# Second-row x turned by VectorE and exchanged through HBM at five stage boundaries, in place of TensorE transposes

## Chip, cores and metric

One core of one Trainium2 chip runs the whole program. The metric is device time in microseconds, the median of several runs. Before the change: 942.03 us, median of 3 runs (939.99 to 943.75).

## The reference

A two-layer decoder trunk on x of 256 rows by 1024 columns, all in float32. Each layer does

```
h = h + 0.5 * swiglu(rms_norm(h, g1), w_gate, w_up, w_down)     # FFN, inner width 2816
h = h + mixer(rms_norm(h, g2))
h = h + 0.5 * swiglu(rms_norm(h, g3), w_gate, w_up, w_down)
```

The mixer of layer 0 is causal differential attention (w_qkv 1024 x 3072, w_o 1024 x 1024). Between the layers one shared K/V is made from rms_norm(h, kv_norm). The mixer of layer 1 is sliding-window attention with sinks (w_q, w_o 1024 x 1024) that reads it. A last rms_norm gives the output.

## The kernel before

The 256 rows are two blocks of 128: pos 0, the first rows, and pos 1, the second rows. Four FFNs, the QKV projection, two attentions, the shared K/V and the w_q and w_o projections run one after the other. Weights come in 157 units of 128 x 2048 elements (1 MB); four are held in SBUF (UNITS_HELD). To get float32 accuracy each operand is split in a high part (float32r) and a low part: ScalarE copies raw into w_hi (L1192), VectorE subtracts to get w_lo (L1536), and TensorE sums three products, hi*hi, hi*lo and lo*hi. One pass over one unit for one block of rows in `columns_pass` (L427) is 12 matmuls of 128x128 by 512 columns. The order of all work is written out by hand for each engine, and each engine runs strictly in that order; semaphores join them. SyncE issues all loads from one queue: the load of unit u waits until VectorE has split unit u-4.

TensorE contracts over partitions, so x must be turned: xT_hi and xT_lo hold the 1024 columns on partitions, 8 tiles by 256 rows. At the end of a stage, VectorE adds the block's result to x (`residual`, L1567) and multiplies by the norm's gain (`gained`, L1557, writes xn and raises s_xn). TensorE transposes xn in eight 128x128 pieces into two PSUM banks (`x_transposes`, L482), ScalarE copies the banks to xT_hi (`x_hi`, L1217), and VectorE writes xT_lo (`x_lo`, L1542). The factor 1/rms comes in later, with the silu, the bias or the copy of the projection.

At each boundary u0 is the first weight unit of the next stage. TensorE first runs the first rows over u0 to u0+3, four passes, and then the second rows over the same units. The second rows' result of the old stage is done only when the new stage begins, so their residual, gain, transposes and parts are made while TensorE runs the first rows' four passes. The transposes stand behind the third of these passes, and `x_ready` before the first pass of the second rows. VectorE's order there is residual(1), split u0+2, split u0+3, gained(1) (`boundary`, `next_phase`).

Before the third FFN (U_FFN1_1) two normalisations of the same x are turned, one for the shared K/V (kept in the hT buffers) and one for the FFN. `kv_pass` (L599) makes K and V with 24 matmuls of 256 columns for each block.

The FFN's inner activations h are turned in another way already. VectorE transposes h in 32x32 blocks (`h_turned`, L1599, STREAM_TRANSPOSE of 128x512 into the silu buffer), SyncE writes 256 KB to a buffer in HBM (`h_out`, L878), waits for its landing, and reads it back with four transfers of 64 KB into xn, one for each group of 32 partitions (`h_in`, L886). ScalarE then copies to hT_hi (L1238) and VectorE makes hT_lo (L1607). The loads of later units stand between these transfers in SyncE's order.

Of the kernel before, what the change touches and what calls it, by code (L numbers as in the profile page):

```python
# [30 lines left out]
F32 = mybir.dt.float32  # L31
# [7 lines left out]
P = 128  # L39
# [87 lines left out]
def trunk(nc, a, out):  # L127
    with ExitStack() as ctx:
# [3 lines left out]
        def sem(name):  # L132
            return ctx.enter_context(nc.semaphore(name))
# [77 lines left out]
        landed = [xn[:, pos, 0:BANK] for pos in range(NPOS)]  # L211

# [42 lines left out]
        s_hT_lo = [sem(f"s_hT_lo{i}") for i in range(NPOS)]  # L255
        s_hipart = sem("s_hipart")
# [132 lines left out]
        def _(pe):  # L389
# [401 lines left out]
            for part in range(3):  # L791
                u0 = U_QKV + 4 * part
                for pos in range(NPOS):
                    for i in range(4):
                        if part == 0 and pos == 0 and i == 3:
                            x_transposes("ln_mix_0", 1)
                        if part == 0 and pos == 1 and i == 0:
                            x_ready("ln_mix_0", 1)
# [39 lines left out]
            for pos in range(NPOS):  # L838
                for i in range(4):
# [4 lines left out]
                    if pos == 0 and i == 3:  # L844
                        x_transposes("ln_mix_1", 1)
                    if pos == 1 and i == 0:
                        x_ready("ln_mix_1", 1)
# [18 lines left out]
        def _(sp):  # L866
# [21 lines left out]
            def ffn(f, u0, w_gate, w_up, w_down, l, *vectors):  # L888
# [18 lines left out]
                for k in range(2 if f == 0 else 0, 8):  # L907
                    unit(u0 + k, k % 2, CH * (k // 2))

# [49 lines left out]
            def columns(u0, n_chunks, w):  # L959

                view = w.rearrange("(k p) n -> p k n", p=P)
                for c in range(n_chunks):
                    for half in range(2):
                        u = u0 + 2 * c + half
                        dst = raw[:, slot(u), :].rearrange("p (k n) -> p k n", k=4)
                        load(u, [(dst[:, 2 * i:2 * i + 2, :],
                                  view[:, 4 * half + 2 * i:4 * half + 2 * i + 2, BANK * c:BANK * (c + 1)])
                                 for i in range(2)])

# [21 lines left out]
            ffn(0, U_FFN1_0, a["ffn1_w_gate"], a["ffn1_w_up"], a["ffn1_w_down"], 0, "ln_mix_0", "ln_ffn2_0", "kv_norm")  # L991
            columns(U_QKV, 6, a["a_w_qkv"][0])
            rows(U_WO_A, 4, a["a_w_o"][0])
            vector("ln_ffn1_1")
            ffn(1, U_FFN2_0, a["ffn2_w_gate"], a["ffn2_w_up"], a["ffn2_w_down"], 0, "ln_mix_1")
# [3 lines left out]
            ffn(2, U_FFN1_1, a["ffn1_w_gate"], a["ffn1_w_up"], a["ffn1_w_down"], 1, "b_b_q", "b_b_o")  # L999
            columns(U_WQ, 2, a["b_w_q"][0])  # L1000
            rows(U_WO_B, 4, a["b_w_o"][0])
            vector("ln_ffn2_1")
            ffn(3, U_FFN2_1, a["ffn2_w_gate"], a["ffn2_w_up"], a["ffn2_w_down"], 1, "final_norm")
# [174 lines left out]
        def _(act):  # L1178
# [43 lines left out]

            def ffn(f, u0, name, aside=None):
# [21 lines left out]
                def turn_of(g, turn=None):  # L1245
                    if g == 0:
                        if name == "ln_ffn1_1":
                            x_hi("kv_norm", 1)
                        x_hi(name, 1)
                    silu_gate(0, 1, g, turn)  # L1250
                    split(u0 + 4 * g + 4, turn)
# [144 lines left out]
            x_hi("ln_mix_0", 1)  # L1396
            projection(0, 0, 1, q_a[:, 0, BANK:D])
            split(U_QKV + 4)
# [85 lines left out]
            x_hi("ln_mix_1", 1)  # L1484
            transposed(qT[:, 0:4, own(0)], 4, ("qT_b", 0, 0))
            split(U_WO_B)
# [35 lines left out]
        def _(dve):  # L1522
# [35 lines left out]

            def residual(key, pos, scale, u_last):
# [11 lines left out]
            def boundary(key, u_last, u0, name, scale=0.5):  # L1571
# [14 lines left out]
            def ffn(f, u0, name):  # L1586
# [28 lines left out]
                def turn_of(g, turn=None):  # L1615
                    if g == 0:
                        if name == "ln_ffn1_1":
                            x_lo("kv_norm", 1)
                        x_lo(name, 1)
                    mul(0, 1)  # L1620
                    if g == 0 and name == "ln_ffn1_1":
# [130 lines left out]
            def next_phase(layer, u0, name):  # L1752
# [11 lines left out]
                residual(("wo", layer), 1, 1.0, u0 - 1)  # L1764
                split(u0 + 2)
                split(u0 + 3)
                gained(name, 1, ("wo", layer))
# [47 lines left out]
            x_lo("ln_mix_0", 1)  # L1815
# [83 lines left out]
            x_lo("ln_mix_1", 1)  # L1899
            queries(0, 1)  # L1900
            split(U_WO_B)
# [67 lines left out]
```

## Time and profile before

| | |
|---|---|
| median of 3 runs | 942.03 us (939.99 to 943.75) |
| the profiled execution | 941.22 us, its span 939.3 us |
| PE busy | 925.9 us, 99% |
| DVE, ACT, POOL busy | 556.7, 459.9, 87.0 us (59%, 49%, 9%) |
| PE L482, all transposes | 2.7% of the chain that ended last |
| DMA | 193.37 MB, 206 GB/s mean |
| mean granted TensorE clock | 0.997 |

PE is TensorE's matmuls, PEld its weight loads, DVE VectorE, ACT ScalarE, POOL GpSimd, and SPq SyncE's queue of DMA issues. A timeline row has the start in us, the duration, the engine, the line of the kernel, the operation, output and input, and in brackets the idle time before it with what ended it. A matmul row shows 0.39 us although the next one starts 0.227 us later: matmuls are pipelined, so starts are to be compared, not durations.

### The profile page before, as it was taken

The page shows a single profiled execution, that of the slowest core. Times are in us where ns is not written, and L with a number is a line of the kernel's source. Part 1 is how long each engine was busy: PE and PEld are TensorE (multiplying, and loading weights), DVE is VectorE, ACT ScalarE, POOL GpSimd, SP SyncE. Part 2 cuts the span into 40 slices and gives each one's busy share as a digit, 9 for nine tenths or more (in the row PEclk, how much of TensorE's full clock was granted, in tenths as well). Part 3 has the DMA queues.
Part 4 walks back from the last instruction along what each step waited for, and adds up shares of the span by engine and source line. Part 5 has one row for each costly group of instructions (what it writes and reads, how often), then busy time and mean ns, then how long its engine had stood idle before and what let it go on. Part 6 is the DMA issues. An engine that isn't in the chain of part 4 may idle for free.

```text
span 939.3 us, 11549 instructions
## 1 busy us (share of the span) xinstructions
PE 925.9 (99%) x4338; PEld 759.6 (81%) x4338; DVE 556.7 (59%) x537; ACT 459.9 (49%) x581; POOL 87.0 (9%) x168
## 2 busy tenths in 40 slices
PE   8999999999999999999999999999999999999996
PEld 7878888888877888888888888888876788888885
DVE  5566663554587666664466666644568766666542
ACT  6354643455676544444343445443447654444431
POOL 1510000024311100000004000000031010000000
PEclk9999999999999999999999999999999999999998
DMA  9798884554532678885564788864641468888521
GB/s 313 190 311 264 293 280 177 179 179 179 202 106 76 191 246 251 251 280 197 188 207 146 227 247 254 306 208 180 217 163 51 129 191 251 248 242 290 201 77 45
DMA packets 149947, 193.37 MB, mean 206 GB/s; under 512 B 8712, under 2 KB 121376, under 8 KB 149904
## 3 DMA queue, kind: packets, MB, share of 16 engines
q1 hardware_dynamic: 149568, 192.45, 62.4%
q0 software_dynamic: 320, 0.34, 0.5%
q8 instruction: 28, 0.46, 0.2%
q14 instruction: 15, 0.12, 0.0%
q10 hardware_dynamic: 16, 0.00, 0.0%
HBM read 181.22 MB, written 11.53 MB: 205 GB/s over the span
## 4 chain that ended last, share of the span: by engine, by line
PE 90%; DMA 3%; ACT 3%; DVE 3%; SPq 1%; POOL 1%; issue 0%; POOLq 0%; DVEq 0%; ACTq 0%
PE bank L427 54%; PE bank L464 20%; PE bank L468 10%; PE bank L482 3%; DMA h_bounce<-silu 2%; DMA raw<-in_ffn_w_up 1%; DVE w_lo L1536 1%; ACT w_hi L1192 1%; PE bank L622 1%; PE bank L599 1%; PE bank L675 1%; ACT silu L1330 0%; ACT h L1330 0%; PE bank L653 0%; ACT w_hi L1344 0%; SPq L886 0%
## 5 line engine op out<-in xcount | busy, mean ns | idle before, releaser
L1536 DVE TENSOR_TENSOR w_lo<-raw,w_hi 128x2048 fp32r<-128x2048 f32 x154 | 351.8, 2293 | 191.2 <-ACT w_hi L1192 191.1
L1192 ACT ACTIVATE w_hi<-raw 128x2048 fp32r<-128x2048 f32 x154 | 295.3, 1919 | 178.4 <-PE bank L468 87.6
L427 PE MATMUL bank<-w_hi,xT_hi 128*128 128x512 f32 x832 | 326.1, 392 | 1.8 <-DVE w_lo L1536 0.8
L427 PE MATMUL bank<-w_hi,xT_lo 128*128 128x512 f32 x832 | 324.0, 389 | 0.0
L427 PE MATMUL bank<-w_lo,xT_hi 128*128 128x512 f32 x832 | 323.9, 389 | 0.0
L427 PEld LDWEIGHTS bank<-w_hi,xT_hi 128*128 128x128 f32 x832 | 156.2, 188 | 36.4 <-issue 2.2
L427 PEld LDWEIGHTS bank<-w_hi,xT_lo 128*128 128x128 f32 x832 | 156.2, 188 | 32.7
L427 PEld LDWEIGHTS bank<-w_lo,xT_hi 128*128 128x128 f32 x832 | 156.3, 188 | 31.6
L464 PE MATMUL bank<-w_hi,hT_hi 128*128 128x512 f32 x348 | 136.4, 392 | 0.0
L464 PE MATMUL bank<-w_lo,hT_hi 128*128 128x512 f32 x348 | 135.4, 389 | 0.0
L468 PE MATMUL bank<-w_hi,hT_lo 128*128 128x512 f32 x348 | 107.2, 389 | 0.0
L468 PEld LDWEIGHTS bank<-w_hi,hT_lo 128*128 128x128 f32 x348 | 65.3, 188 | 13.7
L1238 ACT ACTIVATE hT_hi<-xn 128x512 f32 (+1 forms) x40 | 25.0, 625 | 104.7 <-DMA xn<-h_bounce 104.7
L464 PEld LDWEIGHTS bank<-w_hi,hT_hi 128*128 128x128 f32 x348 | 65.3, 188 | 13.3
L464 PEld LDWEIGHTS bank<-w_lo,hT_hi 128*128 128x128 f32 x348 | 65.4, 188 | 13.2
L1591 DVE SCALAR_TENSOR_TENSOR h<-bank,rstd,silu 128x256 f32<-128x256 f32 x88 | 42.0, 479 | 43.5 <-ACT silu L1232 43.5
L1031 POOL TENSOR_SCALAR ms<-ss 128x1 f32<-128x1 f32 x13 | 5.6, 429 | 668.8 <-ACT junk L1210 668.7
L1232 ACT ACTIVATE silu<-bank,rstd 128x256 f32<-128x256 f32 x88 | 40.2, 460 | 49.1 <-PE bank L427 49.0
L1607 DVE TENSOR_TENSOR hT_lo<-xn,hT_hi 128x512 f32 (+1 forms) x40 | 27.6, 689 | 51.2 <-ACT hT_hi L1238 51.2
L1210 ACT ACTIVATE junk<-x 128x1024 bf16<-128x1024 f32 x13 | 13.7, 1050 | 44.1 <-DVE x L1567 44.0
L1567 DVE SCALAR_TENSOR_TENSOR x<-bank,x 128x512 f32<-128x512 f32 x22 | 14.2, 686 | 31.9 <-PE bank L468 31.9
L1599 DVE STREAM_TRANSPOSE silu<-h 128x512 f32<-128x512 f32 x40 | 28.4, 711 | 1.3
(157 smaller groups left out, 579.1 us busy)
## 6 DMA issues: line engine op xcount, KB each, us to landing
raw<-in_ffn_w_down SPq DMA_DIRECT2D x88, 512.0 KB, 5.1
raw<-in_ffn_w_gate SPq DMA_DIRECT2D x86, 512.0 KB, 4.6
raw<-in_ffn_w_up SPq DMA_DIRECT2D x86, 512.0 KB, 6.0
raw<-in_a_w_qkv SPq DMA_DIRECT2D x24, 512.0 KB, 4.7
h_bounce<-silu SPq DMA_DIRECT2D x40, 256.0 KB, 5.8
xn<-h_bounce SPq DMA_DIRECT2D x160, 64.0 KB, 3.3
raw<-in_a_w_o SPq DMA_DIRECT2D x8, 512.0 KB, 3.9
raw<-in_b_w_q SPq DMA_DIRECT2D x8, 512.0 KB, 5.3
```

What stands on the lines that cost most here:

```text
L427: mm = nc.tensor.matmul(bank[b][:, :], xs[:, kt, own(pos)], ws[:, slot(u), cols], start=(kt == 0 and i == 0), stop=(kt == KT - 1 and i == 2))
L464: nc.tensor.matmul(bank[acc(pos, j)][:, :], lhs_hi[:, kt, own(pos)], ws[:, slot(u), cols], start=(kt == 0 and i == 0), stop=False)
L468: mm = nc.tensor.matmul(bank[acc(pos, j)][:, :], lhs_lo[:, kt, own(pos)], w_hi[:, slot(u), cols], start=False, stop=(kt == n_kt - 1))
L482: mm = nc.tensor.transpose(bank[b][:, P * i:P * (i + 1)], src, ident[:, :])
L1192: nc.scalar.activation(w_parts(u)[0], raw[:, slot(u), :], ACT.Copy).then_inc(s_hi, 1)
L1232: nc.scalar.activation(silu_of(pos, j, g), bank[acc(pos, j)][:, 0:CH], ACT.Silu, scale=rstd[:, pos:pos + 1]).then_inc(s_silu, 1)
L1238: nc.scalar.activation(hT_hi[:, bass.ds((g + turn) * 4, 4), own(pos)].rearrange("p t (q s) -> p t q s", q=4), landed[pos].rearrange("p (q ...
L1536: nc.vector.tensor_tensor(lo, raw[:, slot(u), :], hi.bitcast(F32), ALU.subtract).then_inc(s_lo, 1)
L1567: nc.vector.scalar_tensor_tensor(out=x[:, pos, cols], in0=bank[acc(pos, j)][:, :], scalar=scale, in1=x[:, pos, cols], op0=ALU.mult, op1=AL ...
L1591: nc.vector.scalar_tensor_tensor(out=h[:, pos, CH * j:CH * (j + 1)], in0=bank[b][:, CH:2 * CH], scalar=rstd[:, pos:pos + 1], in1=silu_of(p ...
L1599: nc.vector.transpose(turned[pos].rearrange("p (q t s) -> p t q s", q=4, t=4), h[:, pos, :].rearrange("p (t q s) -> p t q s", t=4, q=4)).t ...
L1607: nc.vector.tensor_tensor(hT_lo[:, tile, own(pos)].rearrange("p t (q s) -> p t q s", q=4), landed[pos].rearrange("p (q t s) -> p t q s", q ...
```

## The change

At five boundaries (ln_mix_0, ln_ffn2_0, ln_ffn1_1, ln_mix_1, ln_ffn2_1) the second rows are turned the way h is. VectorE works on halves of 512 columns: `turned_half` multiplies half a row block by the gain into xn and transposes its 32x32 blocks, half 0 into silu's second block and half 1 into h's. SyncE (`x_moved`) waits for a half, writes it to x_bounce in HBM, waits for the landing, and issues four reads into xn; then the same for the other half. This stands behind the load of u0+3 in SyncE's order, ahead of that of u0+4. ScalarE (`moved_hi`) and VectorE (`moved_lo`) make the parts of each half from xn, and TensorE waits for each half separately (`second_rows_ready`), half 0 before the first pass of the second rows and half 1 before the second. VectorE's order becomes residual(1), turned_half 0, split u0+2, turned_half 1, split u0+3. The first rows, the first FFN's input and the K/V normalisation (kv_norm) are still transposed by TensorE.

```diff
+        x_turned = [silu[:, 1, :, :].rearrange("p j n -> p (j n)"), h[:, 1, :]]
+        x_bounce = nc.dram_tensor("x_bounce", (2, P, BANK), F32).ap()
+        x_landed = [xn[:, 1, BANK * j:BANK * (j + 1)] for j in range(2)]
+        MOVED = ["ln_mix_0", "ln_ffn2_0", "ln_ffn1_1", "ln_mix_1", "ln_ffn2_1"]
...
+            def second_rows_ready(name, j):
+
+                pe.wait_ge(s_x_lo, 2 * MOVED.index(name) + j + 1)
...
                     columns_pass(u0 + 4 * g + 2, 0, 0, 1, ("gu", f, g, 1), turn)
-                    if g == 0:
-                        if name == "ln_ffn1_1":
-                            x_transposes("kv_norm", 1)
-                        x_transposes(name, 1)
+                    if g == 0 and name == "ln_ffn1_1":
+                        x_transposes("kv_norm", 1)
                     columns_pass(u0 + 4 * g + 3, 1, 0, 1, ("gu", f, g, 1), turn)
                     if g == 0:
                         if name == "ln_ffn1_1":
                             kv_pass(1)
-                        x_ready(name, 1)
-                    gate_up(4 * g, 1, 0, g, turn)
+                        for half in range(2):
+                            second_rows_ready(name, half)
+                            columns_pass(u0 + half, half, 1, 0, ("gu", f, 0, 0))
+                    else:
+                        gate_up(4 * g, 1, 0, g, turn)
...
+            def x_moved(name):
+
+                m = MOVED.index(name)
+                for j in range(2):
+                    sp.wait_ge(s_x_turned, 2 * m + j + 1)
+                    sp.dma_start(x_bounce[j], x_turned[j]).then_inc(s_x_bounced[j], 16)
+                    sp.wait_ge(s_x_bounced[j], 16 * (m + 1))
+                    src = x_bounce[j].rearrange("(a i) (q n) -> q i a n", a=4, q=H_READS)
+                    for q in range(H_READS):
+                        dst = x_landed[j][32 * q:32 * (q + 1), :].rearrange("p (a n) -> p a n", a=4)
+                        sp.dma_start(dst, src[q]).then_inc(s_x_landed[j], 16)
...
                 for k in range(2 if f == 0 else 0, 8):
                     unit(u0 + k, k % 2, CH * (k // 2))
+                    if f and k == 3:
+                        x_moved(name)
...
+            def moved_hi(name, j):
+
+                act.wait_ge(s_x_landed[j], 16 * H_READS * (MOVED.index(name) + 1))
+                nc.scalar.activation(xT_hi[:, 4 * j:4 * j + 4, own(1)].rearrange("p t (q s) -> p t q s", q=4),
+                                     x_landed[j].rearrange("p (q t s) -> p t q s", q=4, t=4),
+                                     ACT.Copy).then_inc(s_hipart, 1)
...
+            def turned_half(name, j, key):
+
+                in_sbuf(dve, (*key, 1, 1))
+                v, n = vec_of(name)
+                dve.wait_ge(s_vec[v], n)
+                cols = slice(BANK * j, BANK * (j + 1))
+                ins = nc.vector.tensor_tensor(xn[:, 1, cols], x[:, 1, cols], vec[:, v, cols], ALU.mult)
+                if j == 0:
+                    link(ins)
+                else:
+                    ins.then_inc(s_xn, 1)
+                    dve.wait_ge(s_xn, xn_count(name, 1))
+                nc.vector.transpose(x_turned[j].rearrange("p (q t s) -> p t q s", q=4, t=4),
+                                    xn[:, 1, cols].rearrange("p (t q s) -> p t q s", t=4, q=4)
+                                    ).then_inc(s_x_turned, 1)
...
                 residual(key, 1, scale, u_last)
+                turned_half(name, 0, key)
                 split(u0 + 2)
+                turned_half(name, 1, key)
                 split(u0 + 3)
-                gained(name, 1, key)
...
             dve.wait_ge(s_used, U_KV + 1)
             dve.wait_ge(s_rstd, rstd_count("kv_norm", 0))
             add_bias(kvb[:, 0, :], 0, acc(0, 1), 2 * KVW, bkv[:, :])
+            turned_half("ln_ffn1_1", 0, ("down", 1))
             split(U_FFN1_1 + 2)
             gained("kv_norm", 1, ("down", 1))
-            gained("ln_ffn1_1", 1, ("down", 1))
+            turned_half("ln_ffn1_1", 1, ("down", 1))
             split(U_FFN1_1 + 3)
```

## Rows read from the trace of the kernel before

**Rows 1.** Page: TensorE's busy line; one kind of load with its time to landing.
```profile
PE 925.9 (99%) x4338; PEld 759.6 (81%) x4338; DVE 556.7 (59%) x537; ACT 459.9 (49%) x581; POOL 87.0 (9%) x168
...
raw<-in_a_w_qkv SPq DMA_DIRECT2D x24, 512.0 KB, 4.7
```

**Rows 2.** TensorE's timeline at the boundary before QKV: stage's first matmul, transposes, second after.
```profile
193.58 0.39 PE L427 MATMUL bank<-w_hi,xT_hi 128*128 128x512 f32 x1
...
201.75 1.03 PE L482 MATMUL bank<-ident,xn 128*128 128x128 f32 x8
...
202.85 0.40 PE L427 MATMUL bank<-w_lo,xT_hi 128*128 128x512 f32 x1
```

**Rows 3.** VectorE's timeline at the same boundary.
```profile
193.78 1.29 DVE L1567 SCALAR_TENSOR_TENSOR x<-bank,x 128x512 f32<-128x512 f32 x2 [0.85 <-PE bank L468]
194.99 4.49 DVE L1536 TENSOR_TENSOR w_lo<-raw,w_hi 128x2048 fp32r<-128x2048 f32 x2
199.39 1.22 DVE L1557 TENSOR_TENSOR xn<-x,vec 128x1024 f32<-128x1024 f32 x1
```

**Rows 4.** Groups by line and form: busy us, mean ns of one, idle before.
```profile
L1536 DVE TENSOR_TENSOR w_lo<-raw,w_hi 128x2048 fp32r<-128x2048 f32 x154 | 351.8, 2293 | 191.2 <-ACT w_hi L1192 191.1
...
L1192 ACT ACTIVATE w_hi<-raw 128x2048 fp32r<-128x2048 f32 x154 | 295.3, 1919 | 178.4 <-PE bank L468 87.6 <-PE bank L427 87.0 <-DMA raw<-in_ffn_w_up 3.6
...
L1599 DVE STREAM_TRANSPOSE silu<-h 128x512 f32<-128x512 f32 x40 | 28.4, 711 | 1.3
...
L1607 DVE TENSOR_TENSOR hT_lo<-xn,hT_hi 128x512 f32 x24 | 16.6, 690 | 29.5 <-ACT hT_hi L1238 29.5
...
L1238 ACT ACTIVATE hT_hi<-xn 128x512 f32 x24 | 15.0, 626 | 61.9 <-DMA xn<-h_bounce 61.9
```

**Rows 5.** Timelines of VectorE and TensorE where TensorE waited for a split, first FFN.
```profile
58.47 2.29 DVE L1536 TENSOR_TENSOR w_lo<-raw,w_hi 128x2048 fp32r<-128x2048 f32 x1 [0.94 <-ACT w_hi L1192]
...
60.89 0.49 PE L427 MATMUL bank<-w_hi,xT_hi 128*128 128x512 f32 x1 [0.56 <-DVE w_lo L1536]
61.22 0.40 PE L427 MATMUL bank<-w_lo,xT_hi 128*128 128x512 f32 x1
```

**Rows 6.** Before the third FFN: VectorE's timeline, then the chain (start, us, what).
```profile
492.16 2.28 DVE L1536 TENSOR_TENSOR w_lo<-raw,w_hi 128x2048 fp32r<-128x2048 f32 x1
494.36 0.48 DVE L1583 SCALAR_TENSOR_TENSOR shared<-bank,rstd,bkv 128x256 f32<-128x256 f32 x1
...
493.80 8.19 PE bank L427 x36
501.99 1.75 PE bank L482 x16
```

**Rows 7.** Boundary before w_q, timelines: VectorE's residual, TensorE's transposes, ScalarE's split of w_o.
```profile
679.47 1.29 DVE L1567 SCALAR_TENSOR_TENSOR x<-bank,x 128x512 f32<-128x512 f32 x2 [0.84 <-PE bank L468]
...
687.92 1.03 PE L482 MATMUL bank<-ident,xn 128*128 128x128 f32 x8
...
695.02 1.91 ACT L1192 ACTIVATE w_hi<-raw 128x2048 fp32r<-128x2048 f32 x1 [2.24 <-PE bank L427]
```

**Rows 8.** Issue to landing: L878 at 346.0; L886 at 134.64; L1009; all of L886.
```profile
DMA to landing us min/median/max: 2.0/2.0/2.0
...
134.64 1.75 SPq L886 DMA_DIRECT2D xn<-h_bounce  x4
...
DMA to landing us min/median/max: 1.8/1.9/2.0
...
DMA to landing us min/median/max: 2.6/2.6/2.7
...
DMA to landing us min/median/max: 1.8/3.3/7.8
```

**Rows 9.** SyncE's issue of u0+4; busy time, granted clock, DMA share and GB/s of one stretch.
```profile
189.04 0.88 SPq L873 DMA_DIRECT2D raw<-in_a_w_qkv  x2
...
215.00:220.00 5.00, 5.00 (x24) 4.14 (x23) 4.17 (x3) 3.19 (x3) 4.63 (x5) 1.00 1.02 373
```

More of the change, by code:

```diff
@@ L255, in trunk @@
         s_hT_lo = [sem(f"s_hT_lo{i}") for i in range(NPOS)]
+        s_x_turned = sem("s_x_turned")
+        s_x_bounced = [sem(f"s_x_bounced{i}") for i in range(2)]
+        s_x_landed = [sem(f"s_x_landed{i}") for i in range(2)]
+        s_x_lo = sem("s_x_lo")
         s_hipart = sem("s_hipart")
@@ L794, in _ @@
                     for i in range(4):
[L795 to L798, printed above, removed]
+                        if part == 0 and pos == 1 and i < 2:
+                            second_rows_ready("ln_mix_0", i)
                         if (part, pos, i) == (2, 1, 3):
@@ L843, in _ @@
                                     for g in range(2) for t in range(NPOS)], 4, ("kT",))
[L844 to L847, printed above, removed]
+                    if pos == 1 and i < 2:
+                        second_rows_ready("ln_mix_1", i)
                     columns_pass(U_WQ + i, i % 2, pos, i // 2, ("q_b", i // 2))
@@ L990, in _ @@
             load_x(0)
-            ffn(0, U_FFN1_0, a["ffn1_w_gate"], a["ffn1_w_up"], a["ffn1_w_down"], 0, "ln_mix_0", "ln_ffn2_0", "kv_norm")
-            columns(U_QKV, 6, a["a_w_qkv"][0])
+            ffn(0, U_FFN1_0, "ln_ffn1_0", a["ffn1_w_gate"], a["ffn1_w_up"], a["ffn1_w_down"], 0, "ln_mix_0", "ln_ffn2_0", "kv_norm")
+            columns(U_QKV, 6, a["a_w_qkv"][0], "ln_mix_0")
             rows(U_WO_A, 4, a["a_w_o"][0])
             vector("ln_ffn1_1")
-            ffn(1, U_FFN2_0, a["ffn2_w_gate"], a["ffn2_w_up"], a["ffn2_w_down"], 0, "ln_mix_1")
+            ffn(1, U_FFN2_0, "ln_ffn2_0", a["ffn2_w_gate"], a["ffn2_w_up"], a["ffn2_w_down"], 0, "ln_mix_1")
             dst = raw[:, slot(U_KV), :].rearrange("p (k g c) -> p k g c", k=KT, g=2)
@@ L998, in _ @@
                         for i, w in enumerate(("kv_w_k", "kv_w_v"))])
[L999 to L1000 removed]
+            ffn(2, U_FFN1_1, "ln_ffn1_1", a["ffn1_w_gate"], a["ffn1_w_up"], a["ffn1_w_down"], 1, "b_b_q", "b_b_o")
+            columns(U_WQ, 2, a["b_w_q"][0], "ln_mix_1")
             rows(U_WO_B, 4, a["b_w_o"][0])
             vector("ln_ffn2_1")
[L1003 removed]
+            ffn(3, U_FFN2_1, "ln_ffn2_1", a["ffn2_w_gate"], a["ffn2_w_up"], a["ffn2_w_down"], 1, "final_norm")
             sp.wait_ge(s_xn, xn_count("final_norm", 0))
@@ L1395, in _ @@
             projection(0, 0, 0, q_a[:, 0, 0:BANK])
-            x_hi("ln_mix_0", 1)
+            moved_hi("ln_mix_0", 0)
             projection(0, 0, 1, q_a[:, 0, BANK:D])
+            moved_hi("ln_mix_0", 1)
             split(U_QKV + 4)
@@ L1483, in _ @@
             transposed(kT_b.rearrange("p g s -> p (g s)"), 4, ("kT",))
-            x_hi("ln_mix_1", 1)
+            moved_hi("ln_mix_1", 0)
             transposed(qT[:, 0:4, own(0)], 4, ("qT_b", 0, 0))
+            moved_hi("ln_mix_1", 1)
             split(U_WO_B)
@@ L1557, in gained, with moved_lo @@
                 nc.vector.tensor_tensor(xn_of(name, pos), x[:, pos, :], vec[:, v, :], ALU.mult).then_inc(s_xn, 1)
+            def turned_half(name, j, key):
[12 more added lines that the diff above has]
+                                    ).then_inc(s_x_turned, 1)
+            def moved_lo(name, j):
+                dve.wait_ge(s_hipart, t.next("hipart"))
+                hi = xT_hi[:, 4 * j:4 * j + 4, own(1)].rearrange("p t (q s) -> p t q s", q=4)
+                nc.vector.tensor_tensor(xT_lo[:, 4 * j:4 * j + 4, own(1)].rearrange("p t (q s) -> p t q s", q=4),
+                                        x_landed[j].rearrange("p (q t s) -> p t q s", q=4, t=4),
+                                        hi.bitcast(F32), ALU.subtract).then_inc(s_x_lo, 1)
             def residual(key, pos, scale, u_last):
@@ L1814, in _ @@
             dve.wait_ge(s_table, TABLES)
-            x_lo("ln_mix_0", 1)
+            moved_lo("ln_mix_0", 0)
+            moved_lo("ln_mix_0", 1)
             for i in range(4, 12):
@@ L1898, in _ @@
             queries(0, 0)
-            x_lo("ln_mix_1", 1)
+            moved_lo("ln_mix_1", 0)
             queries(0, 1)
+            moved_lo("ln_mix_1", 1)
             split(U_WO_B)
```

17 lines of the change are left out of this document (12 added, 5 removed).

## The prediction

> **What bounds the kernel now.** I read the page first. The PE line says 99% busy over the 939.3 us span [rows 1]. The reader should see that every other engine has slack on average and that TensorE is the engine whose work must shrink. Next comes TensorE's timeline at a stage boundary, here the end of the first FFN [rows 2]. Passes follow each other without an idle mark: from 193.58 to 201.75 there are 36 matmuls, 0.227 us each, so one pass of 12 takes 2.72 us. Then stand the eight transposes of the second rows, and the second matmul behind them starts at 202.85, where it would have started at 201.98 without them. The transposes thus cost 0.87 us of TensorE's time. At the boundary before the third FFN, where two normalisations are turned, the chain has 1.75 us for sixteen, the same price [rows 6].
>
> Third, VectorE's timeline at that boundary [rows 3], because it makes both the transposes' input and the low halves of the weights that TensorE waits for. I count time from t = 0, TensorE's first matmul of the new stage (193.58). The residual of the second rows starts at 0.20, the two weight splits of u0+2 and u0+3 follow at once and end at 5.9, and only then is the second rows' x multiplied by its gain. That order matters: u0+2 is wanted at t = 5.44 (its split ends at 3.7) and u0+3 at 8.16.
>
> **What is removed.** Eight transposes at each of five boundaries: 5 x 0.87 = 4.35 us. That is the ceiling, and it is 0.46% of the time. About 0.5% (4.7 us) is what a measurement of this kernel can tell from no change, so even the full gain lies within it. The copies out of PSUM (ScalarE's high part, VectorE's low part) stay, with another source; both kinds cost about the same from SBUF [rows 4].
>
> **VectorE's new order.** Between the residual and the splits now stand half a gain multiplication and a 128x512 transpose, twice. The rows for the parts are 0.69 (two SBUF inputs, 128x512), 0.71 (the turn of h) and 2.29 (a split) [rows 4]; where nothing is waited for, starts come 0.08 before the end of the one before [rows 3]. So: residual until 1.49; half 0 multiplied until 2.21 and turned until 2.95; u0+2 split until 5.16 (wanted 5.44, in time); half 1 multiplied until 5.77 and turned until 6.51; u0+3 split until 8.71. It is wanted at 8.16. What such a delay costs shows near the start of the trace, where TensorE waited for a split [rows 5]: the split ended at 60.76, the first matmul came 0.13 later, and the next one 0.33 behind instead of 0.227, 0.10 more. The price is 0.55 + 0.13 + 0.10 = 0.78 us, nearly all that the transposes give back. This holds at three boundaries (ln_mix_0, ln_ffn2_0, ln_ffn2_1), whose order is the same: 3 x (0.87 - 0.78) = 0.27 us of gain.
>
> Before the third FFN the rows differ [rows 6]: split of u0+1 from 492.16, the K/V bias until 494.84, then half 0 (to 496.2), u0+2 (to 498.4), the gain for the shared K/V (1.2), half 1 (to 500.95), u0+3 until 503.16. TensorE wants it at 493.80 + 8.19 + 0.87 = 502.86. Late by 0.30, price 0.53, gain 0.34. At ln_mix_1 four transposes of K stand between the passes, so u0+3 is wanted at 687.92, and the same chain from 679.47 ends at 687.98 [rows 7]: price 0.29, gain 0.58.
>
> **The exchange.** No boundary of the trace shows it, so I bound it by the h exchange of the FFN, same shapes. With nothing else in flight a 256 KB write lands 2.0 us after its issue and the four reads, issued within 1.75, land 1.8 to 2.0 after theirs [rows 8]. The other end is the kernel's last writes, 2.6, and the median of all h reads, 3.3, most of them behind weight loads [rows 8]. I take the short end. SyncE itself holds back the weight loads while it waits here, and those of u0 to u0+3 landed long before, so the queue is empty. Half 0: turned 2.95, written 4.97, reads issued until 6.75. Half 1 (turned 6.51) is then written by 8.8, its reads are issued until 10.5, the last lands at 12.0. ScalarE's high part (0.63, behind the silu or the projection that ends near 12.3) and VectorE's low part (0.69) end at 13.6 [rows 4]. TensorE, 0.78 late, starts the second rows' first pass at 11.66 and wants half 1 at 14.38. Spare: 0.65 us after the 0.13 of the hand-over, so no cost, but it is thin. Half 0, ready near 9.8, is not tight. In the other two boundaries other TensorE work (the K/V pass, or q's transposes and scores) widens it.
>
> The Trainium skill, "DMA: Bandwidth & Descriptors", Anatomy of one DMA, has about 2.0 us fixed plus bytes/436e3 us, fitted on the other issue path: 2.6 us for 256 KB. The landing of 2.0 [rows 8] is shorter; by the page's figure two writes would use up the spare and the sum would lose its gain.
>
> **SyncE's queue.** Behind the new waits stand the loads of u0+4 to u0+7, which now go out from t = 10.5 instead of from 4.5 before t = 0 (189.04) [rows 9]. Issue to landing of a QKV load is 4.7 us [rows 1], the second half starts 0.4 later, and four units then arrive 2.8 us apart (1.05 MB at 373 GB/s) [rows 9]: at 15.6, 18.4, 21.3, 24.1. With 1.92 and 2.29 for the two splits [rows 4], u0+4 is ready at 19.8, wanted at 22.6; u0+7 at 28.3, or 28.8 behind a silu, wanted at 30.7. Hidden, by TensorE's eight passes on the units held. If that cover were gone each us would count in full. The h transfer behind them lands some 2 us later, against several us in which ScalarE waits for TensorE anyway. One place has no slack: at ln_mix_1 the load of the first w_o unit lands near 694.6 to 695.0, and ScalarE splits it at 695.02 now, on the chain that leads into attention [rows 7]; it would want it 0.58 earlier. I book half of that gain as lost, 0.3.
>
> **Sum.** 0.27 + 0.34 + 0.58 - 0.3 = 0.9 us. The profiled execution took 941.22 us (span 939.3 and 1.9 around it), 0.8 below the median of 942.03. So 940.3 for that execution, and 941.1 for the median.
>
> **Rivals.** (1) *Exchange late, slower.* If a write takes 2.6 and a read 2.7, half 1 is ready at 13.6 + 1.2 + 0.8 = 15.6, 1.35 after the 14.25 at which it would still be in time, and with the 0.10 of a restart that costs 1.45 at three boundaries: -0.9 + 4.4 = +3.5, 945.5. It decides from 0.65 us over my figures. For it: two halves overlap in the queue. Against: the idle landings are the same each time. With reads at 3.3 it is 3 x 0.6 more, 947.3.
> (2) *VectorE's delay does not bite*, because transpose and multiplication overlap more, or TensorE's queue hides the late split. Then all 4.35 us come: 937.7. Against: the wait in [rows 5] was not hidden.
> (3) *Weights late.* The four units come as one burst, with h behind them. If the burst runs at the 206 GB/s that are the mean of the span and not at 373, a unit takes 5.1 us and not 2.8, u0+7 is ready 6.9 later, and TensorE loses 5 at each of three boundaries: 956. Against: nothing else is queued, and the burst rate is a row of this stage.
> (4) *TensorE is the cheaper place.* The Trainium skill, "VectorE: DVE Perf Modes", Rules for kernel authors, gives a 128x128 transpose to TensorE where PSUM will do. Mechanism here: the two turns and split halves keep VectorE 2.8 us longer before u0+3. If each turn takes 0.5 more than the row of h because of its other source layout, each of five boundaries loses 1.0: 946.1. By the rows the two prices cancel.
>
> **How the numbers follow.** Forecast 0.57 (own range 939.5 to 942.5); rival 1 0.18; rival 2 0.10; rival 3 0.05; rival 4 0.10. Leaving out rival 3, what of rivals 1 and 4 lies above 946 and the very bottom, 0.2 in all, gives 937.7 to 946.0. Faster by over 0.5% means below 937.3: 0.03, the edge of rival 2. Slower by over 0.5%, above 946.7: rival 3 and a quarter of rivals 1 and 4, 0.12. Within: 0.85.
>
> **What would show it.** TensorE's waits of the new kernel: five waits of L427 for w_lo of about 0.3 to 0.6 idle at the fourth pass (forecast), none (rival 2). Waits for xT_lo at the second pass of the second rows: none (forecast), about 1.4 us three times (rival 1). ScalarE waiting for raw loads near t = 20 with TensorE idle at the ninth to twelfth pass: rival 3. A turn of xn well over 0.71: rival 4. The forecast is wrong if any of these waits exceeds 1 us, or if the matmul cadence is not 0.227 at granted clock 1.00 [rows 9].

## The result

The changed kernel takes 944.14 us (median of 16 runs, 942.06 to 947.81), the kernel before 941.10 beside it (16 runs, 939.94 to 943.75). The ratio is 1.0033 with a 95% interval of 1.0023 to 1.0043: slower by 3.0 us between the medians, where 0.9 faster was forecast. The profiled execution has a span of 942.4 us against 939.3. The time lies inside the range and inside the 0.5% that was called "within", but it moved the other way, as rivals 1, 3 and 4 would have it.

From the page of the changed kernel, the lines that answer to [rows 1]: TensorE is 1.3 us less busy in a span 3.1 us longer, and the loads for QKV take 5.6 us to land instead of 4.7.

```profile
PE 924.6 (98%) x4298; PEld 754.6 (80%) x4298; DVE 564.8 (60%) x552; ACT 460.1 (49%) x581; POOL 86.9 (9%) x168
...
raw<-in_a_w_qkv SPq DMA_DIRECT2D x24, 512.0 KB, 5.6
```

The work that went is there to see (40 matmul records fewer). Where the time went to stands in TensorE's waits of the changed kernel, from 64 us on (line, releaser, us in total, times, longest). The kernel before has one such wait of its passes there, 0.24 us in the first FFN.

```profile
PE bank L435 <- DVE w_lo L1572: 2.1, 5, 0.5
PE bank L435 <- DVE xT_lo L1615: 1.6, 2, 1.3
```

Such a row counts idle time behind the modelled end of a matmul, and a matmul's record outlasts the start of the next. So I read starts. This is TensorE's timeline at the boundary before QKV, which answers to [rows 2]:

```profile
201.88 0.39 PE L435 MATMUL bank<-w_hi,xT_lo 128*128 128x512 f32 x1
202.65 0.50 PE L435 MATMUL bank<-w_hi,xT_hi 128*128 128x512 f32 x1 [0.39 <-DVE w_lo L1572]
202.99 0.39 PE L435 MATMUL bank<-w_lo,xT_hi 128*128 128x512 f32 x1
...
208.00 0.39 PE L435 MATMUL bank<-w_hi,xT_lo 128*128 128x512 f32 x1
209.66 0.50 PE L435 MATMUL bank<-w_hi,xT_hi 128*128 128x512 f32 x1 [1.27 <-DVE xT_lo L1615]
210.00 0.39 PE L435 MATMUL bank<-w_lo,xT_hi 128*128 128x512 f32 x1
```

At the fourth pass two gaps of 0.77 and 0.34 stand where 0.227 each would do: 0.54 + 0.11 = 0.65 us. At the second half of the second rows it is 1.43 + 0.11 = 1.54. In the same way I priced every stall of the five boundaries but one: the 0.70 before the second attention is no gap between matmuls but the gain that does not arrive, and it is read from ScalarE (see *The held loads* below). The stages are measured from one second-row residual of VectorE (L1567 before, the first row of [rows 3]) to the next, the last one to the first-row residual of the fourth FFN. Spans are not compared, because the first FFN, whose code is the same in all kernels here, varies by 3.6 us from profile to profile (its second-row residual starts between 192.9 and 196.5 us).

| stage from the boundary | transposes gone | late split of u0+3 | half 1 late | weights late | sum | stage after - before |
|---|---|---|---|---|---|---|
| QKV, attention 1 | -0.87 | 0.65 | 1.54 | 0 | +1.32 | +1.42 |
| FFN 2 | -0.87 | 0.65 | 0 | 0.40 | +0.18 | +0.27 |
| K/V, FFN 3 | -0.87 | 0.69 | 0 | 0 | -0.18 | -0.16 |
| w_q, attention 2 | -0.87 | 0.16 | 0 | 0.70 | -0.01 | -0.01 |
| FFN 4 | -0.87 | 0.65 | 0.56 | 0.75 | +1.09 | +1.16 |
| all | -4.35 | 2.80 | 2.10 | 1.85 | +2.40 | +2.68 |

The sum and the stage agree to 0.1 us everywhere; before the second attention they do so in part by construction, and the run without exchange below checks that entry on its own. Another 0.36 us of the profile's 3.1 came in the first FFN, ahead of anything changed.

**VectorE's side** came as worked out. Its timeline before QKV answers to [rows 3]; the first two columns are start and duration, and the stage's first matmul is at 193.94.

```profile
194.14 1.29 DVE L1627 SCALAR_TENSOR_TENSOR x<-bank,x 128x512 f32<-128x512 f32 x2 [0.85 <-PE bank L476]
195.47 0.69 DVE L1601 TENSOR_TENSOR xn<-x,vec 128x512 f32<-128x512 f32 x1
196.19 0.71 DVE L1607 STREAM_TRANSPOSE silu<-xn 128x512 f32<-128x512 f32 x1
196.83 2.25 DVE L1572 TENSOR_TENSOR w_lo<-raw,w_hi 128x2048 fp32r<-128x2048 f32 x1
199.00 0.68 DVE L1601 TENSOR_TENSOR xn<-x,vec 128x512 f32<-128x512 f32 x1
199.71 0.71 DVE L1607 STREAM_TRANSPOSE h<-xn 128x512 f32<-128x512 f32 x1
200.35 2.25 DVE L1572 TENSOR_TENSOR w_lo<-raw,w_hi 128x2048 fp32r<-128x2048 f32 x1
203.03 0.72 DVE L1615 TENSOR_TENSOR xT_lo<-xn,xT_hi 128x512 fp32r<-128x512 f32 x1 [0.43 <-ACT xT_hi L1251]
208.91 0.69 DVE L1615 TENSOR_TENSOR xT_lo<-xn,xT_hi 128x512 fp32r<-128x512 f32 x1 [5.17 <-ACT xT_hi L1251]
```

u0+3 is split at 202.60, t = 8.66 (8.71 was forecast). The turn of xn takes 0.71, as that of h. But half 1's low part starts at 208.91, t = 15.0, and not at 12.9.

**The exchange.** SyncE's issues of half 1's four reads, and the loads behind them in its timeline, with the reads' time from issue to landing between:

```profile
L907 SPq DMA_DIRECT2D xn<-x_bounce x4: 303/432/433, 203.0 to 204.3; - x4
DMA to landing us min/median/max: 1.9/2.2/4.0
...
204.73 2.30 SPq L882 DMA_DIRECT2D raw<-in_a_w_qkv  x3
```

Three reads land in 1.9 to 2.2 us, near the 1.8 to 2.0 of [rows 8]. The last one, issued 0.5 before the first of the held loads, needs 4.0. At the fourth FFN another transfer was slow: half 1's write took 3.2 us to land (2.0 to 2.2 at the other boundaries), and its issue on SyncE 1.42 instead of 0.43.

```profile
L902 SPq DMA_DIRECT2D x_bounce<-h x1: 1420/1420/1420, 759.9 to 759.9; - x1
...
DMA to landing us min/median/max: 3.2/3.2/3.2
```

The held loads follow the last read by 0.5 us at every boundary, and at the four others that read lands in 1.9 to 2.0 us all the same. So they are not enough to explain the 4.0. The list of DMA queues shows what the two slow places share: a packet of 16 KB on another queue, named `instruction`, by its name a fetch of program code. The changed kernel's profile has 28 of them on q8. One falls on the slow read before QKV (204.3 to 208.2) and one on the slow write (759.9 to 763.1), in this order, under the page's line for the whole run:

```profile
q8 instruction: 28, 0.46, 0.2%
...
q8 instruction: 1, 0.02, 1.5%
...
q8 instruction: 1, 0.02, 1.8%
```

The same list for the last read in the second FFN (320.2 to 322.2), which landed in 2.0, has SyncE's own queue and no other:

```profile
q1 hardware_dynamic: 487, 0.25, 59.2%
```

Seven kernels here have loads 0.5 us behind a last read, at 35 boundaries in all. In 28 of them no q8 packet starts within 1.5 us of the read's issue, and the read lands in 1.9 to 2.7 us, 2.0 in the median. In the other seven one does, and the read needs 3.0 to 4.0. The packets keep their places: in all seven kernels that exchange both halves, one starts 10.6 to 11.5 us behind the second-row residual before QKV, and one 6.0 to 6.7 behind it in the fourth FFN. Half 1's last read is issued 10.1 behind it in the changed kernel.

**The held loads.** Timelines of ScalarE, VectorE and TensorE in the second FFN (stage's first matmul at 309.83): the split of u0+4 waits for its load until t = 16.5, that of u0+7 until 26.6, and its low part is ready at 30.9, where TensorE wants it at 30.6. The four units land 3.0, 3.0 and 4.1 us apart; ScalarE starts on each as it lands.

```profile
326.37 1.92 ACT L1217 ACTIVATE w_hi<-raw 128x2048 fp32r<-128x2048 f32 x1 [3.53 <-DMA raw<-in_ffn_w_up]
329.39 1.92 ACT L1217 ACTIVATE w_hi<-raw 128x2048 fp32r<-128x2048 f32 x1 [1.09 <-DMA raw<-in_ffn_w_up]
332.40 1.92 ACT L1217 ACTIVATE w_hi<-raw 128x2048 fp32r<-128x2048 f32 x1 [0.73 <-DMA raw<-in_ffn_w_up]
336.44 1.92 ACT L1217 ACTIVATE w_hi<-raw 128x2048 fp32r<-128x2048 f32 x1 [2.12 <-DMA raw<-in_ffn_w_up]
...
338.39 2.29 DVE L1572 TENSOR_TENSOR w_lo<-raw,w_hi 128x2048 fp32r<-128x2048 f32 x1 [1.75 <-ACT w_hi L1217]
...
340.74 0.50 PE L435 MATMUL bank<-w_hi,xT_hi 128*128 128x512 f32 x1
```

Between the last two (332 to 336.5) stands a q8 packet again:

```profile
q8 instruction: 1, 0.02, 1.6%
```

In the fourth FFN no packet falls into the burst and its units land 3.0, 3.0 and 2.9 apart. There the stall comes a loop turn later, at 803.94. Before the second attention ScalarE's split of w_o's first unit waits for its load, 15.55 us behind the residual; before the change it waited for TensorE and came 15.55 behind it as well ([rows 7]), so the gain of TensorE's passes was lost there:

```profile
696.91 1.91 ACT L1217 ACTIVATE w_hi<-raw 128x2048 fp32r<-128x2048 f32 x1 [2.44 <-DMA raw<-in_b_w_o]
```

### The profile page after: what moved, and what is told of

Its sections match the earlier page's. It is cut to its first block, busy times and chain, and to the rows that moved or that the text cites. A ratio compares the mean times of both kernels' runs of the same rounds, so it can differ in the third digit from the quotient of the medians.

```text
span 942.4 us, 11534 instructions
## 1 busy us (share of the span) xinstructions
PE 924.6 (98%) x4298; PEld 754.6 (80%) x4298; DVE 564.8 (60%) x552; ACT 460.1 (49%) x581; POOL 86.9 (9%) x168
## 4 chain that ended last, share of the span: by engine, by line
PE 70%; DMA 12%; DVE 7%; SPq 4%; ACT 3%; issue 2%; POOL 1%; DVEq 0%; POOLq 0%; ACTq 0%
PE bank L435 35%; PE bank L472 20%; PE bank L476 10%; DMA h_bounce<-silu 6%; DVE w_lo L1572 4%; DMA raw<-in_ffn_w_up 3%; PE bank L490 2%; SPq L882 2%; DMA xn<-h_bounce 1%; ACT w_hi L1217 1%; SPq L907 1%; DMA x_bounce<-h 1%; SPq L895 1%; DMA x_bounce<-silu 1%; PE bank L635 1%
## 5 line engine op out<-in xcount | busy, mean ns | idle before, releaser
L1056 POOL TENSOR_SCALAR ms<-ss 128x1 f32<-128x1 f32 x13 | 11.4, 877 | 670.8 <-ACT junk L1235 670.8
```

## Experiments

Theory S says that the loss is this sum of stalls: late split, late half 1, late weights. The q8 packets are in none of the expectations: what is said of them below was read from the same traces, and no run keeps them away. Rival theories stand in each expectation. All times are medians beside the kernel before on the same chip, and "stages" is the sum of the five stages against before, from the profile (+2.68 for the changed kernel).

**No exchange.** Parts made from the turned halves directly, so the 32x32 blocks stand in the wrong places; SyncE does not wait.

```diff
-                act.wait_ge(s_x_landed[j], 16 * H_READS * (MOVED.index(name) + 1))
+                act.wait_ge(s_x_turned, 2 * MOVED.index(name) + j + 1)
...
-                                     x_landed[j].rearrange("p (q t s) -> p t q s", q=4, t=4),
+                                     x_turned[j].rearrange("p (q t s) -> p t q s", q=4, t=4),
...
-                        x_moved(name)
```

> The changed kernel without the trip through HBM: both part-makers read the 32x32-turned halves directly, and SyncE neither waits nor moves them (so the second rows' xT has its blocks in the wrong places; the exchange is the part left out). VectorE's and TensorE's orders are as changed. Theory S (the changed kernel's loss is the sum of its TensorE stalls: 2.1 us from the exchange's second half being late, 1.15 us from weights that were held back, 2.6 us from the late split of u0+3, against 4.35 us of transposes): without exchange and hold only the split's 2.6 remain, so 1 to 1.8 us faster than before, 939.3 to 940.1 where before is 941.1. Rival V (VectorE's extra work and new order cost more than their visible stalls): still slower than before, above 942.

Measured: 940.18 us, ratio 0.9979 (0.9966 to 0.9991), stages -1.42. Rival V falls. The exchange and what it holds back cost 4.1 us of stages, where the table has 3.95 (2.10 + 1.85). Before the second attention the stage is 0.72 shorter than before, and ScalarE's split of w_o's first unit waits for TensorE again, 14.8 us behind the residual (680.89):

```profile
695.70 1.91 ACT L1213 ACTIVATE w_hi<-raw 128x2048 fp32r<-128x2048 f32 x1 [1.70 <-PE bank L435]
```

**No exchange and the splits first.**

```diff
                 turned_half(name, 0, key)
                 split(u0 + 2)
-                turned_half(name, 1, key)
                 split(u0 + 3)
+                turned_half(name, 1, key)
```

> The previous kernel (exchange left out) with VectorE's order changed to residual, half 0, split u0+2, split u0+3, half 1, so that u0+3's low part is ready at about 7.4 us of the stage and is wanted at 8.2. Theory S: the stalls of 0.65 us at three boundaries and about 0.7 and 0.2 at the other two go, and nearly the whole 4.35 us of the transposes come, less what the chain of w_o's first unit keeps: 937.0 to 937.8 where before is 941.1, 2.3 to 2.8 us below the previous kernel. Rival H (TensorE's late fourth pass is made up later in the stage anyway): same as the previous kernel within 0.5 us.

Measured: 937.19, ratio 0.9951 (0.9937 to 0.9965), stages -4.31, that is -0.84, -0.88, -0.88, -0.82 and -0.89. The ceiling of 4.35 is real, and 2.89 us of it hung on VectorE's order alone. Rival H falls. TensorE's one wait of its passes for a split lies at 64 us, in the first FFN, as before the change:

```profile
PE bank L435 <- DVE w_lo L1568: 0.3, 1, 0.3
```

**Only the hold.** The kernel before, with SyncE held where x_moved holds it.

```diff
+            def held(name):
+                for j in range(2):
+                    in_sbuf(sp, ("xT", name, 1, j))
...
+                    if f and k == 3:
+                        held(name)
```

> The kernel before with one wait more: SyncE holds the load of u0+4 at the five boundaries until the second rows' parts are made (some 10.8 us after the stage's first matmul, where x_moved frees the queue in the changed kernel). Everything is computed. Theory S: the held loads cost by themselves what the trace of the changed kernel shows, about 0.4 us in the second and 0.75 us in the fourth FFN, and up to 0.6 at the w_o unit before the second attention: +1 to +1.8 us, 942.1 to 942.9 where before is 941.1. Rival (my blind reading: the hold is hidden by eight passes on held units): 941.1 within 0.4.

Measured: 941.98, ratio 1.0006 (0.9995 to 1.0016). The median decides nothing between theory and rival. The profile shows a stall of 1.0 us at another place than expected, two loop turns into the second FFN, with stages +1.43:

```profile
358.50 0.49 PE L427 MATMUL bank<-w_hi,xT_hi 128*128 128x512 f32 x1 [0.74 <-DVE w_lo L1544]
```

So in this one profile the hold costs something where nothing else is changed, and neither its place nor its size repeats. A q8 packet fell into this burst too (at 324.8; the units landed 4.2, 3.0 and 2.9 apart), and another among the h reads ahead of the stall (349.9), so how much of the 1.0 is the hold's own is open.

**Half 1 wanted later.** At three boundaries the second rows' half 0 is used over u0 and u0+2 before half 1 is waited for. The release of the weight buffers still counts in unit order.

```diff
+                            for half in range(2):
+                                second_rows_ready(name, half)
+                                columns_pass(u0 + half, half, 1, 0, ("gu", f, 0, 0))
+                                columns_pass(u0 + 2 + half, half, 1, 1, ("gu", f, 0, 1), uses_up=2 * half)
```

> The changed kernel with TensorE's order changed at three boundaries (before QKV, second and fourth FFN): the second rows' half 0 is used for both column chunks before half 1 is waited for, so half 1 is wanted 2.7 us later. Theory S: the stalls on the second half (1.54 us before QKV, 0.56 before the fourth FFN) go, the others stay: 2.1 us faster than the changed kernel, 942.0 against its 944.1. If the later release of u0+1's slot makes the weights later, up to 0.7 of it is lost. Rival V: no change from 944.1.

Measured: 942.46, ratio 1.0006 (0.9995 to 1.0016), against the changed kernel's 1.0033. The stage of QKV goes from +1.42 to -0.17: its stall on half 1 was the 1.5 us. Here too a q8 packet fell on half 1's last read (3.5 us to land), and it cost nothing, since half 1 was wanted 2.7 us later. The fourth FFN stays at +1.29, since its late weights (now 0.94 in one stall) took the place of the 0.56. The third, whose order was left, moved from -0.16 to +0.33.

**x_moved behind u0+5.** Likewise for QKV; before the second attention it stands behind the second w_o unit.

```diff
-                    if f and k == 3:
+                    if f and k == 5:
                         x_moved(name)
```

> The changed kernel with x_moved placed two loads later in SyncE's order, behind u0+5 instead of u0+3 (before the second attention behind the second w_o unit). Those two loads may leave before the second rows are turned. Theory S (stalls add up): the weights' stalls (0.40 us in the second FFN, 0.75 in the fourth, about 0.6 on the chain of w_o's first unit) go, the late split and the late second half stay: 1 to 1.7 us faster than the changed kernel, some 1.8 us above before. Rival C (contention): u0+5's load, which leaves within 2 us of the stage's start at the FFN boundaries, delays both halves of the exchange by up to 2 us each, and the kernel gets slower than the changed one by 1 to 3 us.

Measured: 942.10, ratio 1.0006 (0.9993 to 1.0019). No stall on late weights is left (stages 0.03 in the second FFN, -0.72 before the second attention). Late half 1 stays, 0.84 before QKV and 1.54 in the fourth FFN, where it had been 0.56. The stages sum to +1.52, near theory S's 1.8 (the median is 0.8 above the kernel before). Rival C's price, 1 to 3 us slower than the changed kernel, did not come, but a part of its mechanism did: half 0's write needed 2.7 us to land in the second and the fourth FFN and 4.3 in the third, each time with u0+5's load in flight ahead of it. In the fourth FFN a q8 packet on half 0's reads came on top, and before QKV one fell on half 1's last read (3.3).

**Half by TensorE, half by the exchange.**

```diff
-                for j in range(2):
-                    sp.wait_ge(s_x_turned, 2 * m + j + 1)
+                for j in range(1):
+                    sp.wait_ge(s_x_turned, m + 1)
...
+                        half_transposes(name)
```

> The changed kernel with the exchange for half 0 only; half 1 is transposed by TensorE again (four transposes, 0.44 us, behind the fourth pass), and VectorE's order is residual, half 0, split u0+2, split u0+3, half 1. Everything is computed. Theory S: no late split, no late second half, SyncE free at 6.8 us instead of 10.7, so no late weights; half of the transposes' time stays saved: 5 x 0.43 = 2.1 us faster than before, ratio 0.9977. Rival C: the remaining exchange still costs what it gives, ratio 1.000.

Measured: 939.46, ratio 0.9981 (0.9970 to 0.9991), stages -2.07: -0.39, -0.37, -0.42, -0.52, -0.37. Five times the half of 0.87 and no stall. By its stages this is the steadiest of the versions that keep the exchange; half 0's exchange has time to spare.

**Both orders**, VectorE's and TensorE's, first with SyncE as in the changed kernel, then with x_moved behind u0+5 (the diffs above together).

> The changed kernel with VectorE's order residual, half 0, split u0+2, split u0+3, half 1, and TensorE's order of e4 (half 0 for both chunks first) at three boundaries; SyncE as in the changed kernel. Theory S: the late splits go (2.6 us) and half 1 is in time, but SyncE is held 2.2 us longer, so u0+7 and its neighbours, already 0.3 us late in the second FFN, are about 2.5 us later: net between 1 us faster and 4 us slower than before. Rival H (the hold is harmless, as e2 alone seems to say): all of the 4.35 us, ratio 0.9955.

> The previous kernel with x_moved behind the load of u0+5 (both orders and the queue position changed). Theory S: u0+4 and u0+5 land before the exchange, u0+6 and u0+7 leave at 12.8 us and are split by 27 us where they are wanted at 27 and 30: nearly all of the transposes' 4.35 us, 937 to 938 where before is 941.1, ratio 0.996. Rival C: u0+5's load delays the exchange at the FFN boundaries; with half 1 wanted at 16.3 us and ready at 15.5 us without it, up to 1.5 us each at three boundaries, ratio 0.998 to 1.001.

Measured: 948.06, ratio 1.0069 (1.0053 to 1.0086), and 938.66, ratio 0.9972 (0.9961 to 0.9983). The two kernels differ only in how many loads stand ahead of the exchange in one queue, and are 9.4 us apart (stages +7.09 and -3.33). TensorE's waits for splits (us in total, times, longest) in the one and in the other:

```profile
PE bank L435 <- DVE w_lo L1586: 4.5, 5, 1.2
```

```profile
PE bank L435 <- DVE w_lo L1588: 0.2, 1, 0.2
```

And ScalarE's split of u0+5 in the second FFN, first with the hold, then with that load sent ahead: it waits for its load, or for TensorE.

```profile
330.74 1.91 ACT L1231 ACTIVATE w_hi<-raw 128x2048 fp32r<-128x2048 f32 x1 [1.09 <-DMA raw<-in_ffn_w_up]
```

```profile
327.08 1.92 ACT L1233 ACTIVATE w_hi<-raw 128x2048 fp32r<-128x2048 f32 x1 [2.81 <-PE bank L435]
```

Rival H of the first (the hold is harmless) falls, and theory S's bound of 4 us slower was too low. The second beats both the kernel before and the changed one; its ratio lies between theory S's 0.996 and rival C's 0.998. Its stages are -0.81, -0.89, -0.17, -0.88 and -0.58.

**The third FFN's exchange early again.** The second kernel of the pair above (e8) had lost 0.63 there on half 1.

```diff
-                    if f and k == 5:
+                    if f and k == (3 if f == 2 else 5):
```

> e8_orders_k5 with x_moved ahead of u0+4's load again at the third FFN alone, where e8 shows a stall on the second half of 0.63 us at 509.67 while the loads of u0+4 and u0+5 leave in the middle of the exchange. Theory S: that stall goes and the held loads are hidden there as they were in the changed kernel: 0.6 us faster than e8, ratio to before about 0.9966. Rival: another stall takes its place (late weights in the third FFN), ratio 0.997 to 0.998.

Measured: 939.88, ratio 0.9982 (0.9971 to 0.9993), no better than the kernel it came from. The stall on half 1 in the third FFN stayed (0.8), so u0+4's and u0+5's loads in the exchange were not its cause. What both kernels have there is a q8 packet on half 1's last read, which landed in 3.5 us in e8 and in 3.7 here. In the kernel with both orders and the early x_moved the last read landed in 2.0 at this place, behind two reads that a packet had slowed, and the stall was under 0.3. So VectorE's order, by which half 1 is turned behind the split of u0+3, leaves little spare there, and the slow read uses it up. Before QKV and in the fourth FFN half 1 was also late in this profile (0.65 and 0.6), where e8, with the same code at both, had nothing. At both places both profiles have a packet on the reads, with SyncE's issue of one stretched to 1.9 and 1.7 here and to 1.3 in e8. The stage before the second attention went from -0.88 to -0.19: a packet fell on half 1's last read there (3.0 us to land), and ScalarE splits w_o's first unit right behind that half's high part.

**Loads let go only when half 1 has landed.**

```diff
                         sp.dma_start(dst, src[q]).then_inc(s_x_landed[j], 16)
+                sp.wait_ge(s_x_landed[1], 16 * H_READS * (m + 1))
```

> The changed kernel with one more wait: SyncE lets the four held loads go only when the second half's four reads have landed. Theory R (before QKV the last read took 4.0 us to land, and not 2, because the loads issued right behind it shared its DMA engines): the read lands in 2.0, the stall on half 1 before QKV shrinks from 1.54 us to nothing or little; the loads leave 2 us later, so late-weight stalls grow by up to 2 us each at the boundaries where they show. Rival L (the slow landing is chance and has nothing to do with the loads): the half-1 stall stays at 1.5 us in the profile.

Measured: 948.66, ratio 1.0077 (1.0064 to 1.0091). Before QKV the slowest read now lands in 2.8 us and not in 4.0, TensorE has no stall on half 1 there, and the stage is at +0.33 (from +1.42). That seems to speak for theory R, but the trace has another reading. The read that took 2.8 was issued with nothing behind it and with a q8 packet 0.6 us later, so the packet slows a read without the loads. And in the fourth FFN, where a packet falls on half 0's reads again, TensorE still waits for half 1, although the loads are kept back (0.7, start to start). Whether loads behind add to what a packet costs, 4.0 against 2.8, one pair of profiles can't say. The loads, 2 us later still, cost far more: +1.79, +1.36 and +2.42 in the second FFN, the second attention's stage and the fourth FFN.

```profile
L907 SPq DMA_DIRECT2D xn<-x_bounce x4: 303/432/433, 201.7 to 203.0; - x4
DMA to landing us min/median/max: 1.8/2.0/2.8
...
q8 instruction: 1, 0.02, 2.2%
...
PE bank L435 <- DVE xT_lo L1616: 0.4, 1, 0.4
PE bank L435 <- DVE w_lo L1573: 3.0, 6, 1.2
```

**VectorE's new work alone**, in the kernel before, its turned halves read by nobody.

```diff
                 residual(key, 1, scale, u_last)
+                turned_half(name, 0, key)
                 split(u0 + 2)
+                turned_half(name, 1, key)
                 split(u0 + 3)
-                gained(name, 1, key)
```

> The kernel before with VectorE's new work and order at the five boundaries (half multiplied, half turned into a buffer that nobody reads, split u0+2, and so again before u0+3), TensorE's transposes and everything else as before. Theory K (the transposes themselves were the cover: 0.87 us of TensorE between the third and the fourth pass hides the split that ends at 8.7, wanted at 9.0): no loss, 941.1 within 0.5. Rival: the late split costs its 0.65 us at three boundaries whatever TensorE does, +2 us, 943.1.

Measured: 942.41, ratio 1.0005 (0.9993 to 1.0016), stages +0.84 in small parts of 0.1 to 0.3. TensorE waits for no split at any of the five boundaries. At each boundary VectorE comes 2.8 us later to u0+3's split. In the changed kernel that cost 2.80 us over the five boundaries; here, with the transposes still behind the third pass, it is nearly free: the transposes were the cover for the split of u0+3. What the +0.84 is made of is open.

## Why the prediction was right and wrong

*The ceiling.* 0.87 for eight transposes, 4.35 in all: right. The run without exchange and with the splits first gives -4.31.

*VectorE's late split.* Right in mechanism, place and nearly in size. Forecast 0.78 three times, 0.53 and 0.29, 3.16 in all; measured 0.65 three times, 0.69 and 0.16, 2.80 in all. The splits took 2.25 us there and not 2.29, and the hand-over to TensorE was shorter than in [rows 5]. One step of the chain stands in no row that the prediction names: it has a pause of 0.03 us before an operation that reads the result of the one before it. With the 0.08 of overlap that it states, and no pause, u0+3 would have been ready at 8.39 and the price 0.46. The trace has the pause (0.04 and 0.03). Rival 2, that it does not bite, is out.

*The exchange.* Here the first step failed, and the forecast with it: "Spare: 0.65 us ..., so no cost". It rests on "so the queue is empty" and on landings of 2.0 for every transfer. SyncE's queue was empty, but a q8 packet of instructions came by another one, for which the sum had no term. Nine of ten writes (2.0 to 2.2) and most reads (about 2.0) landed as taken. One read of 4.0 and one write of 3.2, each with a packet on it, gave 1.54 and 0.56 us of stall, 2.10 where nothing was booked. One of these waits, 1.27, is the sign of being wrong that the prediction had named. That a packet stands at both is shown; that it is the cause is read from the 35 boundaries above and from no run that keeps it away. The effect is rival 1's, priced at three boundaries and come at two, but not for the reason given there, that all transfers are slow or two halves overlap. The Trainium skill's formula ("DMA: Bandwidth & Descriptors", Anatomy of one DMA) gives an estimate of 2.6 us for such a write; nine of ten stayed below it, the tenth above.

*The held loads.* The second step that failed is "Hidden, by TensorE's eight passes on the units held", with 0.3 booked in all and 1.85 measured. In the second FFN the first unit landed at t = 16.5 and not 15.6, and the fourth at 26.6 and not 24.1. An undisturbed unit came every 3.0 us and not every 2.8, and the fourth, with a packet on it, 4.1 after the third. The spare of 1.9 us at u0+7 met a delay of 2.5; without the packet's 1.1 the 0.40 of stall would by these figures not have come. SyncE's own issues stretched from 0.5 to 1.3 us in this burst, but in the fourth FFN they did so too while the units landed 3.0 apart, so that is a sign of the full queue and not what made the weights late. In the fourth FFN the delay surfaced a loop turn later, beyond where I had looked. Of the w_o unit I had seen that it has no slack, and booked 0.3 where the whole 0.70 went. That is rival 3 in its effect, at a tenth of the price that I gave it and with 0.05 of the chance; the burst did not fall to the mean rate that rival 3 assumed.

*Rival 4*, a dearer turn, is out: 0.71 in the trace. TensorE was the cheaper place all the same, for another reason than the turn's own price.

*The sum.* -0.9 forecast, +2.4 by the same terms measured, of which +2.1 is the exchange, +1.55 the loads and -0.36 the split. The sum had one term, the gain of 4.35, that could only shrink, and three covers of less than 2 us each, all of which I booked in full at one profile's durations. With three covers of that size in series, a cost near zero was not the likeliest case. Without the packets at their places the table would lose up to 2.5 of its 3.95 us for exchange and loads, by this reading, and would have come out near zero. No row of the prediction showed where they would fall.

## What to carry to other kernels

When a step leaves the engine that bounds a kernel, ask first what its time was covering: here the transposes hid a weight split, and their removal gave it back as a wait until the split was put ahead. A wait in an in-order DMA queue is paid by what stands behind it: the loads of two units moved ahead of the exchange were worth 9.4 us of 940, more than twice what the whole change could bring. Where a round trip has only a few tenths of a microsecond to spare, make the consumer want it later, or send half of it. When one transfer is slow, look at the other DMA queues of the profile in that stretch before blaming the neighbours in its own.

## What the runs showed of the hardware

A 64 KB read out of HBM, or a 256 KB write to it, lands in 1.8 to 2.2 us when nothing else is in flight. With 512 KB loads issued 0.5 us behind it in the same queue, a last read still landed in 1.9 to 2.7 (28 cases). Where a 16 KB packet of q8, the queue named `instruction`, started within 1.5 us of the issue, a read needed up to 3.4 with no load close behind, and a last read 3.0 to 4.0 with one (seven cases). In the bursts of the FFNs a unit lands about 3.0 us after the one before; in the second FFN, where a packet falls into the burst of five kernels (at 332.3 in the changed one), the unit that it meets lands 4.1 to 4.2 after. There are 28 packets in 942 us. Half 0's write, issued with loads in flight ahead of it, took 2.4 to 4.3 us in the FFNs of the kernels with x_moved behind u0+5.

SyncE's issue of one 512 KB load went from 0.43 to 0.51 us for the first four of a burst to 1.3 to 1.9 for the sixth to the eighth, without a packet, and to 1.3 for the third with one (205.7). I read this as a full queue holding up the engine that issues into it. A TensorE stall costs some 0.25 us more than its row of idle time says: 0.65 where the row says 0.39, 1.54 where it says 1.27.
